# One unit for eight compressed heads, an inverse level on 64 columns, and other seams in a whole two-model kernel

## What is computed

```python
def first_block(x, ...):
    u = rms_norm(h, norm1_g[i])
    p_rwkv, p_nsa = jnp.split(u @ w_in[i], [N_RWKV_COLS], axis=-1)
    y_rwkv = rwkv7_time_mix(p_rwkv, ...)       # 8 heads of 64
    y_nsa = nsa_attention(p_nsa, ...)          # 8 query heads, 2 key heads
    h = h + concatenate([y_rwkv, y_nsa]) @ w_out[i]
    h = h + swiglu(rms_norm(h, norm2_g[i]), ...)
    return rms_norm(h, norm_f_g)

def step(S, inp):                              # the recurrence, per head
    sa = jnp.einsum('bhvk,bhk->bhv', S, a_t)
    S = S * w_t[...] + sa[..., None] * b_t[...] + v_t[..., None] * k_t[...]
    return S, jnp.einsum('bhvk,bhk->bhv', S, r_t)

# nsa_attention, for each block of 128 queries: three softmaxes, gated and added
#   o_c: 15 compressed keys (n_cmp = 15) made by a small network of 32 tokens each
#   o_s: the selected keys (with 256 tokens all are selected), o_w: the window
return gb[..., 0:1] * o_c + gb[..., 1:2] * o_s + gb[..., 2:3] * o_w

def second_block(x, ...):
    for layer in range(2):
        x = x + 0.5 * swiglu_2(rmsnorm(x, g[0]), ...)
        x = x + (even_mixer if layer % 2 == 0 else odd_mixer)(rmsnorm(x, g[1]), ...)
        x = x + 0.5 * swiglu_2(rmsnorm(x, g[2]), ...)
    return rmsnorm(x, final_norm_g)

# even_mixer: gated linear attention beside attention with a cumulative forget sum
F = jnp.cumsum(log_f, axis=1)
s = s + (Fb.transpose(0, 2, 1)[..., :, None] - F_keys[..., None, :])
```

## Time and profile before

| | |
|---|---|
| median of three runs | 1489.45 us |
| profiled execution, its own time | 1488.83 us |
| its span, mean TensorE clock | 1486.7 us, 0.992 of full |
| PE busy | 1450.2 us, 98% |
| PEld busy | 1332.9 us, 90% |
| DVE busy | 958.1 us, 64% |
| ACT busy | 706.2 us, 48% |
| POOL busy | 86.9 us, 6% |
| chain that ended last | PE 90%, DVE 5%, ACT 3%, issue 2% |
| of it the line of all products, L435 | 87% |

### The profile page before, as it was taken

The page is one execution under the profiler, slowest core; times in us unless marked ns, Lnnn a source line. Parts: engine busy times, 40 slices in busy tenths (PEclk is TensorE's granted clock), DMA queues, the critical chain, the costliest instruction groups (busy, mean ns, idle before and its releaser), DMA issues.

```text
span 1486.7 us, 26239 instructions
## 1 busy us (share of the span) xinstructions
PE 1450.2 (98%) x10328; PEld 1332.9 (90%) x10328; DVE 958.1 (64%) x1577; ACT 706.2 (48%) x1159; POOL 86.9 (6%) x130
## 2 busy tenths in 40 slices
PE   8999999999999999999999999999999999999997
PEld 7887988899998999989988999999999878899997
DVE  4765545776666866666557666676666666676665
ACT  6753443544335434446665434354443656444342
POOL 2040001000002000010000000000000114000000
PEclk9999989999999999999999999999999999999999
DMA  8343000555453645433335555445454424355440
GB/s 343 145 149 128 1 2 1 199 217 203 174 195 110 238 180 202 179 128 128 128 128 221 204 187 193 176 165 211 170 200 182 147 89 163 136 209 205 171 169 29
DMA packets 26576, 238.07 MB, mean 160 GB/s; under 512 B 2544, under 2 KB 6784, under 8 KB 7808
## 3 DMA queue, kind: packets, MB, share of 16 engines
q1 hardware_dynamic: 23968, 233.65, 42.2%
q10 hardware_dynamic: 2528, 3.32, 0.7%
HBM read 235.89 MB, written 1.07 MB: 159 GB/s over the span
## 4 chain that ended last, share of the span: by engine, by line
PE 90%; DVE 5%; ACT 3%; issue 2%; POOL 1%; DMA 0%; ACTq 0%; DVEq 0%; POOLq 0%
PE ps L435 87%; DVE w_gu L1919 1%; PE ps L816 1%; DVE uT_l L1876 1%; PE ps L895 1%; DVE ring_r L1912 0%; DVE x L1938 0%; PE ps L439 0%; DVE ring_r L2270 0%; ACT uT_h L1241 0%; PE ps L1022 0%; DMA cst<-consts_in 0%; ACT wk L1419 0%; POOL small L1766 0%; POOL small L1767 0%
## 5 line engine op out<-in xcount | busy, mean ns | idle before, releaser
L435 PE MATMUL ps<-uT_h,w_gu 128*128 128x256 f32 x3520 | 614.3, 280 | 0.3
L435 PEld LDWEIGHTS ps<-uT_h,w_gu 128*128 128x128 f32 x3520 | 537.8, 188 | 11.1 <-issue 1.6
L435 PE MATMUL ps<-uT_l,w_gu 128*128 128x256 f32 x1760 | 478.8, 279 | 0.0
L435 PE MATMUL ps<-w_dn,h_r 128*128 128x512 f32 x1320 | 326.2, 396 | 2.1 <-issue 1.0
L435 PEld LDWEIGHTS ps<-uT_l,w_gu 128*128 128x128 f32 x1760 | 325.5, 188 | 0.0
L435 PEld LDWEIGHTS ps<-w_dn,h_r 128*128 128x128 f32 x1320 | 239.4, 188 | 53.3 <-issue 3.7
L1288 ACT CAST w_gu<-ring 128x2048 fp32r<-128x2048 f32 x110 | 209.9, 1909 | 156.3 <-PE ps L435 155.4
L1919 DVE TENSOR_TENSOR w_gu<-ring,w_gu 128x2048 fp32r<-128x2048 f32 x110 | 252.1, 2292 | 35.3 <-ACT w_gu L1288 35.3
L1949 DVE TENSOR_TENSOR us<-ps,bc 128x256 f32<-128x256 f32 x110 | 46.5, 423 | 202.9 <-PE ps L435 202.8
L1301 ACT ACTIVATE wk<-wk 128x256 f32<-128x256 f32 x110 | 46.1, 419 | 260.3 <-DVE wk L1947 260.3
L1294 ACT CAST w_dn<-ring 128x1024 fp32r<-128x1024 f32 x110 | 115.7, 1052 | 82.6 <-PE ps L435 82.4
(11 more groups left out here) (370 smaller groups left out, 1843.5 us busy)
## 6 DMA issues: line engine op xcount, KB each, us to landing
ring<-wstream SPq DMA_DIRECT2D x144, 1536.0 KB, 6.5
cst<-consts_in SPq DMA_DIRECT2D x1, 2185.0 KB, 13.7
wk<-t_row ACTq DMA_DIRECT2D x1, 2048.0 KB, 8.6
wk<-masks_in SPq DMA_DIRECT2D x1, 1216.0 KB, 23.4
x<-x_in SPq DMA_DIRECT2D x2, 512.0 KB, 4.5
ring<-wstream SPq DMA_DIRECT2D x1, 1024.0 KB, 9.0
inh<-gains ACTq DMA_DIRECT2D x2, 512.0 KB, 9.7
out_dram<-x SPq DMA_DIRECT2D x4, 256.0 KB, 2.2
```

Source lines behind the costliest of these rows:

```text
L435: return pe.matmul(o, l, r, start=start, stop=stop, skip_group_check=True)
```

## The change

- **Compressed branch.** The eight heads' scores over 16 (15 and a pad) keys go side by side into one unit of 128 columns, with four products of 32 columns. VectorE adds the distances, finds a maximum for each head, subtracts it and applies the slopes. ScalarE takes one exp. The value product multiplies with a matrix `Vbd`, 128 by 512, in which each head's rows hold the values, so that one product gives all eight heads. The denominators are summed on VectorE two calls later. Units are now 34, groups end at units 7, 8, 16, 24, 25 and 33 (`NSA_LAST`).
- **Slots.** `NSA_STEPS` gives slot A one call in each step from 2, slot B one call in odd steps only. `nsa_result` stands four calls behind the last unit of its group.
- **Inverse.** `HALF_FROM` goes from 12 to 8.
- **Even mixer.** The sums' products (`fox_sums`) go in pairs between the eight k steps of the item ("tok", 0, 2).
- **Norms 4 and 7.** Squares in four parts, GpSimd adds them as they come, and its memsets wait for the diagonals.
- **Feed-forwards.** A Silu on one column is issued before the first step of the first and the last one, and the first's transfer issue on ScalarE goes behind step 0.
- **End.** The product of row tile 1's first half with the gain stands between the residual parts. That half is scaled on ScalarE, the other on VectorE behind row tile 0, and ScalarE issues its own output transfer.

```diff
-HALF_FROM = 3 * QUADS
+HALF_FROM = 2 * QUADS
-        NSA_STEPS, CMP_FROM, BRANCHES = [0, 0] + [2] * 20 + [3, 3], 6, (1, 0, 2)
+        NSA_STEPS, CMP_FROM, BRANCHES = [0, 0] + [1, 2] * 10 + [1, 1], 6, (1, 0, 2)
...
+                        if b == 0:
+                            units.append(dict(cmp=True, q=[qT[:, j, tk] for j in range(4)], K=P, grp=grp, pos=0, last=True,
+                                              dist=C("alibi_cmp", 16 * t, 16 * t + 16)))
+                            continue
...
+        NSA_LAST = [i for i, a in enumerate(UN["nsa"]) if a["last"]]
-        SQ_PARTS = {n: 3 if n in (0, 4, 7, 9) else 2 for n in range(10)}
+        SQ_PARTS = {n: 4 if n in (4, 7) else 3 if n in (0, 9) else 2 for n in range(10)}
@@ TensorE, steps and nsa(i)
-                    for _ in range(NSA_STEPS[q] - 1):
+                    for _ in range(min(NSA_STEPS[q], 1)):
                         nsa(i)
...
-                    if NSA_STEPS[q]:
+                    for _ in range(NSA_STEPS[q] - 1):
                         nsa(i)
...
+                    if a["cmp"]:
+                        for j in range(4):
+                            last = mm(ps[3 + i % 2][:, 32 * j:32 * j + 32], a["q"][j], kcT[:].rearrange("p g c -> p (g c)"))
+                        last.then_inc(s["S_ps"], 1)
...
+                    if a["cmp"]:
+                        mm(o[:, :], nPT[:, u % 2, 0:P], Vbd.rearrange("p u n -> p (u n)")).then_inc(s["o_ps"], 1)
@@ TensorE, even mixer
+            def fox_sums(h):
+                if h == 0:
+                    pe.wait_ge(s["gk_cs"], 1)
+                for part in range(2):
+                    last = mm(ps[h // 2][:, h % 2 * T:(h % 2 + 1) * T], head_r[0:8, h:h + 1].to_broadcast([8, P]),
+                              fsum_r[part][0:8, :], part == 0, part == 1)
+                if h == 7:
+                    last.then_inc(s["f_ps"], 1)
...
-                    if it == ("tok", 1, 1):
-                        pe.wait_ge(s["gk_cs"], 1)
-                        for h in range(8):
...
@@ ScalarE
+                if norm in (1, 8):
+                    act.activation(small[:, 61:62], C("neg_half", 0, 1), ACT.Silu)
...
+                step(0)
+                if norm == 1:
                     act.dma_start(scratch, t5_row).then_inc(s["t5_out"], 16)
-                step(0)
...
-                    if u % 8 == 0 and u >= 16:
-                        act.wait_ge(s["o_ready"], u // 8 - 1)
+                    if a["pos"] == 0 and a["grp"] >= 2:
+                        act.wait_ge(s["o_ready"], a["grp"] - 1)
+                    if a["cmp"]:
+                        act.activation(nPp[:, u % 3, 0:P], nSS[:, u % 3, 0:P], ACT.Exp).then_inc(s["p_ready"], 1)
...
-            for half in range(2):
-                hs = slice(half * 512, (half + 1) * 512)
-                act.wait_ge(s["rstd_ready"], 2 * 9 + 2)
-                act.wait_ge(s["xg_ready"], half + 1)
-                act.mul(x[:, 1, hs], xn[:, 1, hs], rstd(9)[:, 1:2]).then_inc(s["out1_ready"], 1)
+            act.wait_ge(s["rstd_ready"], 2 * 9 + 2)
+            act.wait_ge(s["xg_ready"], 1)
+            A(act.mul(x[:, 1, 0:512], xn[:, 1, 0:512], rstd(9)[:, 1:2]), "out1_ready")
+            act.dma_start(out[P:2 * P, 0:512], x[:, 1, 0:512]).then_inc(s["stored"], 16)
@@ GpSimd, norm
+                if SQ_PARTS[n] == 4:
+                    for t in range(TT):
+                        gp.wait_ge(s["ss_ready"], SQ0[n] + 2 * t + 1)
+                        G(gp.tensor_scalar(small[:, 9:10], ss4[2 * t], 1.0, 1e-6, ALU.mult, ALU.add))
+                        gp.wait_ge(s["ss_ready"], SQ0[n] + 2 * t + 2)
+                        G(gp.tensor_tensor(o[:, t:t + 1], ss4[2 * t + 1], small[:, 9:10], ALU.add))
+                        G(gp.tensor_tensor(o[:, t:t + 1], o[:, t:t + 1], C("neg_half", 0, 1), ALU.pow), "rstd_ready")
+                    gp.wait_ge(s["diag_ready"], 2 * TN[n] + 2)
+                    return
@@ VectorE
+                    if n == 9 and i == 2:
+                        v.wait_ge(s["gain1"], 16)
+                        V(v.tensor_tensor(xn[:, 1, 0:512], x[:, 1, 0:512], gb[:, 1, 0:512], ALU.mult), "xg_ready")
...
+                if a["cmp"]:
+                    z = nSS[:, i % 3, 0:P].rearrange("p (u c) -> p u c", c=16)
+                    V(v.tensor_tensor(z, ps[3 + i % 2][:, 0:P].rearrange("p (u c) -> p u c", c=16),
+                                      a["dist"].unsqueeze(1).to_broadcast([P, 8, 16]), ALU.add))
+                    V(v.tensor_reduce(cmp_max, z, AX.X, ALU.max))
+                    V(v.tensor_tensor(z, z, cmp_max.unsqueeze(2).to_broadcast([P, 8, 16]), ALU.subtract))
+                    V(v.tensor_tensor(z, z, C("slopes").unsqueeze(2).to_broadcast([P, 8, 16]), ALU.mult), "max_ready")
...
-                if i % 8 == 4 and i > 8:
-                    nsa_result(i // 8 - 1)
+                if i >= 2 and UN["nsa"][i - 2]["cmp"]:
+                    u, g = i - 2, UN["nsa"][i - 2]["grp"] % 2
+                    v.wait_ge(s["p_ready"], u + 1)
+                    V(v.tensor_reduce(den[:, 8 * g:8 * g + 8], nPp[:, u % 3, 0:P].rearrange("p (u c) -> p u c", c=16),
+                                      AX.X, ALU.add))
+                if i - 4 in NSA_LAST:
+                    nsa_result(NSA_LAST.index(i - 4))
...
+                V(v.tensor_tensor(Vbd, ps[5][:, 0:HD].unsqueeze(1).to_broadcast([P, 8, HD]),
+                                  C("head_rows").unsqueeze(2).to_broadcast([P, 8, HD]), ALU.mult), "cmp_v")
```

More of the change, by code:

```diff
@@ L417, in _ @@
                 sp.dma_start(ring[:, i % RING, :], wstream[i]).then_inc(s[f"land{i % RING}"], 16)
-            for t in range(TT):
-                for half in range(2):
-                    sp.wait_ge(s[("out0_ready", "out1_ready")[t]], half + 1)
-                    sp.dma_start(out[t * P:(t + 1) * P, half * 512:(half + 1) * 512],
-                                 x[:, t, half * 512:(half + 1) * 512]).then_inc(s["stored"], 16)
+            for n, (t, half) in enumerate(((0, 0), (0, 1), (1, 1))):
+                sp.wait_ge(s["out0_ready"], n + 1)
+                sp.dma_start(out[t * P:(t + 1) * P, half * 512:(half + 1) * 512],
+                             x[:, t, half * 512:(half + 1) * 512]).then_inc(s["stored"], 16)
             sp.wait_ge(s["stored"], 16 * 2 * TT)
@@ L893, in nsa @@
                     for k in range(0, a["K"], P):
[L894 to L895 removed]
+                        last = pe.transpose(ps[5][:, k:k + P], nPp[:, u % 3, k:k + P], ident)
                     last.then_inc(s["pT_ps"], 1)
@@ L1055, in even_in @@
                         piece(1, 0)
-                    if it == ("tok", 1, 1):
-                        pe.wait_ge(s["gk_cs"], 1)
-                        for h in range(8):
-                            for part in range(2):
-                                last = mm(ps[h // 2][:, h % 2 * T:(h % 2 + 1) * T],
-                                          head_r[0:8, h:h + 1].to_broadcast([8, P]), fsum_r[part][0:8, :],
-                                          part == 0, part == 1)
-                        last.then_inc(s["f_ps"], 1)
             def gla_A(t):
@@ L1222, in squares @@
             def squares(n):
-                parts = [(0, 0, D), (1, 0, 512), (1, 512, D)] if SQ_PARTS[n] == 3 else [(0, 0, D), (1, 0, D)]
+                parts = {2: [(0, 0, D), (1, 0, D)], 3: [(0, 0, D), (1, 0, 512), (1, 512, D)],
+                         4: [(t, lo, lo + 512) for t in range(TT) for lo in (0, 512)]}[SQ_PARTS[n]]
+                sums = ss4 if SQ_PARTS[n] == 4 else ss3 if n == 3 else ss
                 for i, (t, lo, hi) in enumerate(parts):
@@ L1491, in compress_out @@
                 act.wait_ge(s["cmp_kv"], 1)
-                A(act.copy(kcT[0:64, 0, 0:15], ps[6][0:64, 0:15]))
-                A(act.copy(kcT[64:128, 1, 0:15], ps[6][64:128, 15:30]))
-                A(act.copy(vc[0:15, :, :], ps[6][0:15, 64:192].rearrange("p (g d) -> p g d", g=2)), "gate_tok")
+                for g in range(2):
+                    r = slice(HD * g, HD * (g + 1))
+                    A(act.copy(kcT[r, g, 0:NC_CMP], ps[6][r, 16 * g:16 * g + NC_CMP]), "kc_ready" if g else "a_step")
                 act.wait_ge(s["gates_ps"], 1)
@@ L2088, in rwkv @@
                 for q in range((LEVELS - 1) * QUADS):
-                    if q == CMP_FROM - 2:
+                    if q == 2:
                         compress()
-                    for _ in range(NSA_STEPS[q] - 1):
+                    for _ in range(min(NSA_STEPS[q], 1)):
                         nsa(i)
```

148 lines of the change are left out of this document (81 added, 67 removed).

## The result

Over 20 runs of each, the kernel before takes 1482.98 us (1480.48 to 1489.58) and the changed kernel 1497.12 (1489.23 to 1510.76). The ratio is 1.010, with a 95% interval of 1.0082 to 1.0118. The forecast was 1478.4, faster. The three runs known at the prediction all lay near 1489. Most of before's runs lie at 1480.5 to 1484, the rest near 1489. The changed kernel's lie between 1489 and 1511, most of them near 1494, 1499.5, 1503.5, 1506.3 and 1510.6, and the mean granted clock falls as the time grows: 0.996 at 1489.23, 0.993 near 1494, 0.990 near 1499.5, 0.981 at 1510.76.

What follows compares the result with a forecast made beforehand. TensorE, 98% busy in program order, was taken as the bound. Gains 6.9 + 1.8 + 0.7 + 0.6 + 1.0 = 11.0 from 1488.83 leave 1477.8; the runs' median being 0.6 higher, 1478.4 us. Range 1470 to 1488.

Steps and rivals of the forecast that it cites:

- the stage: Recurrence's inverse interleaved with block attention: gain 6.9 us, after stalls of 5.8 and 2.5 for the clock.
- What bounds the kernel: Whole kernel: TensorE, busy 98% of the span, in program order; waits elsewhere count only when its next instruction stands behind them.
- The inverse's work: Inverse steps with attention units: 72.5 us where before took 87.45; 7.9 of the 14.95 less is work.
- The two gaps: Steps 9 and 20 to 21: exp waits for VectorE's result, stalling TensorE 3.0 and about 2.8 us.
- What the gaps do to the clock: Inverse stage: idle gaps of 3 us may make the clock fall; one earlier fall cost 1.7 us.
- I take 2.5 for both: Inverse stage: 2.5 us allowed for clock loss behind both result waits, bounds 0 and rival C.
- Rival C: From step 9's stall the clock stays at half, a step taking about 5.26; to step 19, about 1509 us. Chance 0.18.
- The 7.0 won back: Inverse's last level: low clock expected to go as 256-key units replace 15-key ones; 7.0 us counted whole.
- The sums: Cumulative sums paired between k steps: clock hole's 1.7 goes, seven switches cost some 0.1 each; gain 0.7 us.
- Silu: First and last feed-forward: preloading the activation table removes TensorE idle before the first down products; gain 1.8 us.
- Norms: Norms 4 and 7: squares in four halves, memsets waiting for diagonals; gain 0.6 us (0.4 and 0.2).
- The end: Kernel's end: row tile 1's halves scaled in parallel on ScalarE and VectorE, ScalarE issuing its own output DMA; gain 1.0 us.

Runs made afterwards that it cites:

- the 16-column version: The kernel before with sixteen unused columns more in its table of constants, nothing else changed: 1490.62 us, ratio 1.0051.
- changed with 48 columns: The whole changed kernel with 48 unused columns of constants, weight tiles 256 bytes behind their place in the kernel before: 1486.54 us, ratio 1.0034 to before.

## Why the prediction was wrong

The misses add up: of the 22.1 us between −11.0 and +11.1, 5.2 are in the stage (−1.75 for −6.9), 8.3 at the sums, 8 are the addresses and 0.6 the end.

- **What bounds the kernel** held: every microsecond found above is TensorE slow or idle.
- **The inverse's work** held. With the gaps repaired, P(3) to the product behind the steps is 74.65; the forecast sum was 72.5 without any gap. The kernel before in an execution without its hole (the 16-column version) needs 81.30 for it (141.45 to 222.75). So the work gain is 6.7, forecast 7.9.
- **The two gaps** held: 2.91 and 2.66, forecast 3.0 and 2.8, at the places, with the releaser and by the order that the prediction gave.
- **What the gaps do to the clock** failed first. The step that failed is "I take 2.5 for both", drawn from a hole behind sixteen eight-row products. Behind the first gap the clock was low for 13.4 us, 6.7 us lost; behind the second, over the profiles that have it, for nothing, for 3.4 us, or for 27, at least 13.4 lost. Rival C had the mechanism and its price (a step of 5.26; measured 5.12), and I gave it 0.18. The Trainium skill's page "TensorE: Matmul & The Clock Gate", section "HAM oscillation — how this bites in real kernels", has idle gaps take the clock down. The changed kernel's profile agrees behind the first gap (2.91 idle, then a granted clock of 0.53) and shows nothing of the kind behind the second (2.66 idle, then 1.00).
- **The 7.0 won back** was half a mistake: the profiled execution has the hole and the three runs known then were as long, but most later runs of before are 5 to 9 us shorter (1480.5 to 1484), which fits a hole less. Against those runs that term is 0.
- **The sums** failed in sign. The term was a hole that goes away (1.7) less seven switches at 0.1, which by itself makes 1.0 and not the 0.7 that was put down. In the profiled execution the hole did not go away but was longer (15.5 × 0.44 = 6.8 us lost). In executions with the clock up the pairs still cost 14.76 − 11.44 = 3.3: seven switches at 0.37 make 2.6, and the wait for the split weights, no longer covered, 0.6. No term had that wait. The bound of −1.0 was too near.
- **The addresses** are a term the prediction lacks. `slopes` and `head_rows` are sixteen columns in the constants, ahead of `wk` in SBUF. I priced the edits' instructions and not what the new tiles move. It costs 8.1 by the fastest runs, of before with and without the sixteen columns.
- **Silu** held (1.8). **Norms** held (0.64, forecast 0.6): TensorE's wait for the first diagonal shrank from 1.37 and 1.31 to 1.17, and the 0.30 before norm 4's second diagonal went, since that diagonal took 0.29 and not 0.98. **The end** gave 0.4, not 1.0: counted from the last down product's load group, the last scaled half is ready 0.8 earlier (7.8 and not 8.6), but the end comes only 0.43 earlier. GpSimd's last scale still waits for ScalarE's last squares; why half of the 0.8 is lost behind the scaling stays open.
- The range failed by its upper end, 1488.0: it took rival C and the missing terms as one tenth.

## What to carry to other kernels

Where TensorE is 98% busy, price a new wait twice: its own length, and a stretch at half clock behind it, which here was from nothing to 27 us long and differed between executions. Compare the addresses of the tiles behind every allocation that a change enlarges, because a table of constants grown by 64 bytes cost 8.1 us here, more than the 6.7 that the reworked stage won. Before small products are spread out, see which wait the block was covering. Take the runs before as a distribution, and see which of its kinds the profiled one belongs to.

## What the runs showed of the hardware

- The same products, at a granted clock of 1.00 both, took 116.7 or 118.3 ns each (5.60 and 5.68 us per 48), by whether the weight tile lies 0 or 64 bytes from its old place modulo 256. At 128 bytes they took 117.3 (5.63), at 168 bytes 118.8 (5.70). What moved is all that lies behind the constants, w_gu and w_dn in `wk` among it. The operand that these products stream did not move, so its reading is not the reason. Whether it is TensorE's load of the weights or what else moved stays open. The down products have it the other way round: they stream w_dn, which moved, and load h_r, which did not. Twelve of them took 2.80 at 0 and at 64 bytes, 2.81 at 128 and 2.77 at 168.
- In the 14 profiles the clock fell 18 times between 140 and 1460 us, and the loss (us × missing share of the clock, in windows of 1 us) was 1.7 in ten of these, 6.8 in seven and 13.7 in one, with nothing in between. That is 3.4, 13.7 and 27.3 us at half clock.

| place | clock low for, us, by profile |
|---|---|
| behind the first gap, 64-column products | 13.7 in three of three (the changed kernel, sums in one block, changed with 48 columns) |
| behind the first gap, 128-column products | 3.4 in one of one |
| behind the second gap | none in two, 3.4 in two, 27.3 in one |
| sums in one block | 3.4 in seven, none in two |
| sums in pairs | 13.7 in three, none in one |
| sums in two halves | none in one |
| last level of the kernel before, no gap | 13.7 in one, none in one (the 16-column version) |

- What decides between executions, and between the three lengths, stays open: one program has its clock fall in some executions and not in others.
